# Reordering the memory stage of a fused decoder-layer kernel on all engines

## The chip, the cores and the metric

One NeuronCore of a Trainium2 chip runs the whole kernel in one launch. The metric is the device time of an execution in microseconds; lower is better.

## The reference, cut to what matters

The kernel computes one decoder layer for a prompt of 512 tokens and for 8 samples of one token each, in f32. The change touches the second part of the layer, the attention into a memory of 256 rows, with 4 heads of 256:

```python
def mem_kv(mem, mem_norm, w_mk, w_mv):
    m = rmsnorm(mem, mem_norm)
    return ((m @ w_mk).reshape(B, 256, 4, 256), (m @ w_mv).reshape(B, 256, 4, 256))

def mem_attend(h, mk, mv, w_xq, w_xo):
    q = (h @ w_xq).reshape(B, T, 4, 256)
    s = jnp.einsum('bthd,bmhd->bhtm', q, mk).astype(jnp.float32) * MEM_SCALE
    p = jax.nn.softmax(s, -1).astype(mv.dtype)
    o = jnp.einsum('bhtm,bmhd->bthd', p, mv).reshape(B, T, 1024)
    return o @ w_xo
```

The prompt's keys and values are computed here (and are outputs too). The samples read theirs from caches, 1 MB of keys and 1 MB of values for each sample.

## The kernel before, in words

**Tiling.** Every large matmul is made of three: a weight and its operand are each split into a high part (`whi`, written by ACT with a Copy) and a low part (`wlo`, written by DVE as the difference, L1756), and PE multiplies high by high, low by high and high by low (L2527 to L2529, `mm3`). So each 512 KB block of weights passes through four hands: SP loads it into one of two buffers `wraw` (`load_w`, L893, which waits until DVE has finished the low part of the block before the last), ACT writes `whi` (`split_w`, L1150, which also waits until PE has used the block three before), DVE writes `wlo`, PE multiplies. Each engine has its own list of work, written out by hand in one order, and executes it strictly in that order; semaphores tie the lists together.

**The stage.** After the query projection `xq` (eight tiles, m = 0 to 7) come 16 blocks of memory weights, called blocks 0 to 15 here. `MEM_TILES` gives their order: 0 to 3 are key tiles 0 to 3, 4 and 5 are the two halves of value tile 0, 6 and 7 are key tiles 4 and 5, 8 and 9 value tile 1, 10 and 11 key tiles 6 and 7, 12 and 13 value tile 2, 14 and 15 value tile 3. The split that stands at the head of a tile on ACT and DVE is that of a later block: `key_tile(j)` and `value_tile(h)` call `split_next`, which splits the block two further on. So `key_tile(6)` begins with the split of block 12 and `key_tile(7)` with that of block 13, on ACT and on DVE.

**The prompt's attention**, head by head, h = 0 to 3: `mem_scores(h)` on PE; `cmaxes(h)` on DVE (row maxima, value `cnegm`); `cexps(h)` on ACT; `normalised(h)` on DVE (value `cpn`); `turned(h)`: eight transposes on PE, high part `PTc_hi` on ACT, low part on DVE; `mixed(h)`: PE multiplies the values with the turned probabilities, ACT and DVE split the result into `A_hi` and `A_lo`. `key_rows(h)` turns keys back for the output. In ACT's list `cexps(1)` and `key_rows(1)` stand ahead of `turned(0)`.

**The samples' scores** are made on DVE, `scores_of(g)` for nine groups g = 0 to 8 (`SPREADS`): groups of 6 or 8 products of a cached key row with a query row (L2140). The query rows reach all partitions by DMA: ACT writes the rows of head h to DRAM (`query_rows(h)`, L1171), and POOL, in order of g, broadcasts them into one of four buffers `q_by` (`broadcast_rows`, L1124), once the scores four buffers back are made (`q_spent`). In POOL's list the zeroing of `Pv_pad` (L1135) stands at g = 3 and waits first for PE's sum of squares `("ssq", "nx")`. Scores of groups 0 to 4 stand in the `xq` loop behind the tiles m = 3 to 7, those of groups 5 to 8 behind key tiles 0 to 3. From all scores follows a small chain: `cmx` (maximum, DVE), `cmxt` (transpose, PE), `cdiag` (DVE), `cmxb` (matmul, PE), `cdif` (DVE), the exponential `Pcs` (ACT), `csum` (DVE), `ctot` (PE), `cpnorm` (DVE); then `cached_values(b)` on PE, 16 matmuls for each sample.

**SP's queue.** `load_w` of block i and the cached values share one list. The values V0 to V7 go into slots that held cached keys, so their loads wait: V0 for the scores of group 7 (`spent(sp, 7, 1)`), V1 to V3 for those of group 8 (`spent(sp, 8, 1)`), V4 and V5 for `mem_scores(1)`, V6 and V7 for `cached_values` that have freed a slot. V0 stands behind the load of block 8, V1 to V3 behind blocks 9 to 11, V4 and V5 behind 12 and 13. ACT's `mixed(0)` and `mixed(1)` wait for the scores of group 8 as well, since `A_hi` overwrites those slots.

**PSUM.** Seven banks are handed out in the fixed order of `bank_order`; PE waits for the bank seven places back to be freed.

Of the kernel before, what the change touches and what calls it, by code (L numbers as in the profile page):

```python
# [21 lines left out]
P = 128  # L22
# [3 lines left out]
NB = 8  # L26
# [67 lines left out]
def weight_pieces():  # L94

    o = []
    for j in range(J0, NF):
# [4 lines left out]
SPREADS = [[[(0, 0), (0, 1)], [(0, 2)]], [[(0, 3), (0, 4)], [(0, 5), (0, 6)]],  # L102
# [4 lines left out]
QBUF = 4  # L107

# [21 lines left out]
def bank_order():  # L130
# [59 lines left out]
        if m == 6:  # L190
            o += [("ssq", "nx")]
    o += [("mm", 0), ("qt", 3)] + [("mm", j) for j in (1, 2, 3)]
    o += mem_scores(0) + [("mn", 0)] + [("mv", 0), ("mm", 4), ("cmxt",), ("mm", 5), ("cmxb",)]
    o += mem_scores(1) + [("mn", 1)] + turned(0) + [("mv", 1), ("ctot",)] + mixed(0) + [("mm", 6), ("mm", 7)]
    o += mem_scores(2) + [("mn", 2)] + turned(1) + mem_scores(3) + [("mn", 3), ("mv", 2)] + mixed(1)
    o += turned(2) + [("mv", 3)] + mixed(2) + turned(3) + [("xo", 0, 0), ("cot",)] + mixed(3)
    o += [("xo", m, f) for m in range(KD) for f in (0, 1) if m or f]
    for j in range(J0 - 1):
# [15 lines left out]
def val_order():  # L214

    o = [("gT",), ("xsg",), ("xs1",)] + [("x1", c) for c in range(0, KD, 2)]
    o += [("ms", "n1"), ("n1d",), ("bc",)]
    o += [("ckv", r, f) for r in (0, 1) for f in (0, 1)]
    o += [("krx", f) for f in (0, 1)] + [("gT2",), ("cpT",)]
    o += [("up", g, f) for g in (3, 2) for f in (0, 1)]  # L220
    o += [("kr", f) for f in (0, 1)]
    o += [("ms", "nkv"), ("nkd",)]
    o += [("up", g, f) for g in (1, 0) for f in (0, 1)]
    o += [("c", r, f) for f in (1, 0) for r in (0, 1)]
    o += [("cq", m, f) for m in range(KQ) for f in (0, 1)]
    o += [("ms", "nq"), ("rq",)]
    o += [("qr", p, f) for p in (0, 1) for f in (0, 1)]
    o += [("qs",), ("qls",), ("sprod",)]
    us = units()
    o += [("negm",) + us[0], ("negm",) + us[1], ("negm",) + us[2], ("rs",) + us[0]]  # L230
    for n in range(len(us)):
        o += [("rs",) + v for v in us[n + 1:n + 2]] + [("negm",) + v for v in us[n + 3:n + 4]]
        if n == len(us) - 1:
            o += [("turned", 0)]
    for b in range(1, NB):
        if b in ADDED:
            o += [("xo1", ADDED[b], 0)]
        o += [("turned", b)]
    o += [("bias",), ("own_p",), ("spread_p",), ("xo1", 4, 0), ("rows",), ("xo1", 5, 0)]
    for n, m in enumerate(OUT_ORDER):  # L240
        o += [("xo1", m, f) for f in (0, 1) if f or m >= NFIRST]
        if n == MT_AT - 3:
            o += [("ms", "mem")]
        if n == MT_AT - 2:
            o += [("memn",)]
    o += [("ms", "nxs"), ("rx",), ("ms", "nx"), ("rxp",), ("cnegm", 0), ("cmx",), ("cdiag",), ("cpn", 0), ("cdif",), ("csum",)]
    o += [("cnegm", 1), ("cpn", 1), ("cpnorm",), ("cnegm", 2), ("cnegm", 3), ("cpn", 2), ("cpn", 3)]
    for m in range(KD):
        if m == 3:
            o += [("T13", J0)]  # L250
        if m == 4:
            o += [("T2", J0), ("T4", J0)]
        o += [("xo2", m, f) for f in (0, 1)]
    o += [("ms", "nf", f) for f in (0, 1)]
    for j in range(J0):
        if j == 1:
            o += [("S1",), ("S2",), ("S3",)]
        o += [("gv", j, 0)]
        if j == 0:
            o += [("xg", c) for c in range(0, 4)]  # L260
        if j == 1:
            o += [("S4",)]
        o += [("gv", j, 1)]
        if j == 0:
            o += [("xg", c) for c in range(4, KD)]
        o += [("h", j)]
    for j in range(J0, NF + 1):
        if j + 1 < NF:
            o += [("T13", j + 1), ("T2", j + 1), ("T4", j + 1)]
        if j > J0:  # L270
            o += [("u0", j - 1), ("h", j - 1)]
        if j < NF:
            o += [("u1", j), ("g0", j)]
    for m in range(KD - 1):
        o += [("xo3", m, f) for f in (0, 1)]
        if m in (5, 6):
            o += [("y", t, m - 5) for t in range(5)]
    for g in (0, 1):
        o += [("xo3", KD - 1, g), ("ms", "nz", g), ("z", g)] + [("zs",)] * g + [("yinv", g)]
        o += [("yout", t) for t in Y_GROUP[g] if t % 2 == 0]  # L280
    return o
# [61 lines left out]
def build(nc, a, consts, outs):  # L343
# [4 lines left out]
    with ctx:  # L348
# [531 lines left out]
        def _(sp):  # L880
# [60 lines left out]
            for i in range(2, len(MEM_TILES) + 2):  # L941
# [2 lines left out]
                    full(sp, ("xq", KD - 1, 1))  # L944
                    load_kv(7)
                if i == 8:
                    spent(sp, 7, 1)
                    load_kv(NB)
                elif i in (9, 10, 11):
                    spent(sp, 8, 1)  # L950
                    load_kv(NB + i - 8)
                elif i in (12, 13):
                    full(sp, ("cs", 1, 1))
                    load_kv(NB + i - 8)
                elif i in (14, 15):
                    sp.wait_ge(v_used, i - 13)
                    load_kv(NB + i - 8)
            def load_b(j):

                if j == J0 + 1:  # L960
# [28 lines left out]
        def _(gp):  # L989
# [140 lines left out]

            squares("nx", "xo1", range(KD), lambda c: xT[:, c, :], accx, sqx, between=first_rows)
            for g in range(2, len(SPREADS)):
                if g == 3:
                    full(gp, ("ssq", "nx"))
                    gp.memset(Pv_pad[:, :], 0.0).then_inc(vpad_set, 1)  # L1135
                broadcast_rows(g)
# [4 lines left out]
        def _(act):  # L1141
# [352 lines left out]
            def value_tile(h):  # L1494
# [4 lines left out]
                b = full(act, ("mv", h)).rearrange("p (t c) -> p t c", t=2)  # L1499
                act.activation(dst, b, ACT.Copy).then_inc(v_staged, 1)  # L1500
                if h == 0:
                    spent(act, 7, 1)
                else:
                    freed(act, ("cpv", h - 2, 1)) if h >= 2 else None
                high(("mv", h), mv_hi[:, h % 2, :, :], b)
# [16 lines left out]
            def turned(h):  # L1522
                for mb in (0, 1):
# [1 line left out]
                    if h and mb == 0:  # L1525
                        full(act, ("cpv", h - 1, 1))
                    if h == 0 and mb == 0:
                        spent(act, 7, 1)
                    high(("cpt", h, mb), PTc_hi[:, mb, :], b)

            def mixed(h):
# [15 lines left out]
            value_tile(0)  # L1547
            key_tile(4)
            key_tile(5)
            after(("cdif",))  # L1550
            act.activation(Pcs[:, :, :, :], Dc[:, :, :, :], ACT.Exp, scale=MEM_SCALE).then_inc(c_exp, 1)
            cexps(1)
            key_rows(1)
            turned(0)
# [1 line left out]
            mixed(0)  # L1556
            key_tile(6)
            key_tile(7)
            cexps(2)
            key_rows(2)  # L1560
            turned(1)
# [168 lines left out]
        def _(dve):  # L1730
# [420 lines left out]
            for m in range(KD):  # L2151
# [13 lines left out]
                if m == 6:  # L2165
# [3 lines left out]
                    step(dve.reciprocal(rx[:, 0:4], rx[:, 0:4]))  # L2169
                    dve.tensor_scalar(x_scale[:, 0], rx[:, 0:4], MEM_SCALE, None, ALU.mult).then_inc(rx_made, 1)  # L2170
                    value(("rxp",), dve.tensor_scalar(x_scale[:, 1], rx[:, 0:4], -MEM_SCALE, None, ALU.mult))
                if m >= 3:
                    scores_of(m - 3)


# [36 lines left out]

            for j in range(4):
                key_tile(j)
                if j == 3:
                    split_next(("mv", 0, 0))
                scores_of(5 + j)
            cmaxes(0)
            value(("cmx",), dve.tensor_reduce(cols[:, 3], Sc[:, :, :, :].rearrange("p b j h -> p b h j"), AX, ALU.max))
            split_next(("mv", 0, 1))  # L2220
            b = full(dve, ("cmxt",))
            top = cols[0:NB * NH, 2].rearrange("p b h -> p (b h)")[:, 0:1]
            frees(dve.reduce_max(top, b[0:NB * NH, 0:P], AX), ("cmxt",))
            freed(dve, ("cmxt",))
            value(("cdiag",), dve.tensor_scalar(diag[0:NB * NH, :], ident[0:NB * NH, 0:NB * NH], top, None, ALU.mult))
            value_tile(0)
            normalised(0)
            key_tile(4)
            key_tile(5)
            b = full(dve, ("cmxb",))  # L2230
            frees(dve.tensor_copy(cols[:, 3].rearrange("p b h -> p (b h)"), b[:, 0:NB * NH]), ("cmxb",))
            freed(dve, ("cmxb",))
            value(("cdif",), dve.tensor_tensor(Dc[:, :, :, :], Sc[:, :, :, :], inner(cols[:, 3], 2), ALU.subtract))
            dve.wait_ge(c_exp, 1)
            value(("csum",), dve.tensor_reduce(cols[:, 6], Pcs[:, :, :, :].rearrange("p b j h -> p b h j"), AX, ALU.add))
            cmaxes(1)
            turned(0)
            value_tile(1)
            normalised(1)
            mixed(0)  # L2240
            ins = dve.reciprocal(cols[:, 7].rearrange("p b h -> p (b h)"), full(dve, ("ctot",))[:, 0:NB * NH])
            frees(ins, ("ctot",))
            freed(dve, ("ctot",))
# [1 line left out]
            own_column = Pv_pad[:, 0:NB * (VW + 1)].rearrange("p (b x) -> p b x", x=VW + 1)[:, :, 0:VW]  # L2245
            value(("cpnorm",), dve.tensor_tensor(own_column.rearrange("p b (j h c) -> p b j h c", j=2, h=NH)[:, :, :, :, 0],
                                                 Pcs[:, :, :, :], inner(cols[:, 7], 2), ALU.mult))
            key_tile(6)
            key_tile(7)
            cmaxes(2)  # L2250
            turned(1)
            cmaxes(3)
            normalised(2)
# [247 lines left out]
        def _(pe):  # L2501
# [545 lines left out]
            key_rows(0)  # L3047
            value_tile(0)
            key_tile(4)
            b = out(("cmxt",))  # L3050
            after(("cmx",))
            filled(pe.transpose(b[0:NB * NH, 0:P], cols[:, 3].rearrange("p b h -> p (b h)"), ident[:, :]), ("cmxt",))
            key_tile(5)
            b = out(("cmxb",))
            after(("cdiag",))
            filled(pe.matmul(b[:, 0:NB * NH], ones[0:NB * NH, :], diag[0:NB * NH, :], start=True, stop=True), ("cmxb",))
            mem_scores(1)
            key_rows(1)
            turned(0)
            value_tile(1)  # L3060
            b = out(("ctot",))
            after(("csum",))
            filled(pe.matmul(b[:, 0:NB * NH], ones[:, :], cols[:, 6].rearrange("p b h -> p (b h)"), start=True, stop=True), ("ctot",))
            mixed(0)
            key_tile(6)
            key_tile(7)
            cached_values(0)
            mem_scores(2)
            key_rows(2)
            cached_values(1)  # L3070
            turned(1)
            mem_scores(3)
            key_rows(3)
            cached_values(2)
            cached_values(3)
            value_tile(2)
            mixed(1)
            cached_values(4)
            turned(2)
            value_tile(3)  # L3080
            cached_values(5)
            mixed(2)
# [203 lines left out]
```

## Time and profile before

| | us |
|---|---|
| three runs | 814.67, 818.43, 821.01 |
| median | 818.43 |
| the profiled execution, its own time | 817.74 |
| its span, first to last instruction | 815.9 |
| granted clock of PE, mean over the span | 0.986 |

The profiled execution lies 0.69 us below the median. Its span leaves 1.84 us outside. Times in rows are microseconds from the start of the span. A granted clock of 1.00 is 2.4 GHz; the lower of its two levels is 1.2 GHz, which would show as 0.50, so a mean between them is a mixture.

### The profile page before, as it was taken

To read this page: it belongs to the slowest core of one execution; us is meant where nothing else is said; L and a number is where in the kernel's file an instruction comes from. 1 tells how busy PE (TensorE), PEld (TensorE's weight loads), DVE (VectorE), ACT (ScalarE), POOL (GpSimd) and SP (SyncE) were. 2 spreads that over 40 slices of the span, in tenths; PEclk is the share of its full clock that TensorE was granted. 3 is DMA by queue.
4 is the path that set the end of the run, shared out by engine and by line. 5 is a ranking of instruction groups with operands and counts; after the bars stand their busy time and mean duration, and the time that the engine had idled before them with its cause. 6 is when DMAs were issued, how large, how long until landed. Compare 5 with 4: busy or idle time off the path is not lost. (4 is left out here: it accounts for less than half of the span.)

```text
span 815.9 us, 15998 instructions
## 1 busy us (share of the span) xinstructions
PE 770.4 (94%) x6304; PEld 736.3 (90%) x6304; DVE 550.2 (67%) x1092; ACT 378.2 (46%) x817; POOL 126.0 (15%) x179
## 2 busy tenths in 40 slices
PE   6999988988999988889999998999999999999995
PEld 6998877865899988878799998999999999999995
DVE  5678664678566779756379889888888879222323
ACT  5524775512264433655334345555555567122313
POOL 0376302331004821000046000000000000000000
PEclk9999998999999998999999999999999999999998
DMA  9323332544496658894243231433333331432312
GB/s 271 103 53 92 91 106 69 215 155 156 129 327 223 196 160 241 284 358 155 78 127 104 66 90 57 121 107 110 112 105 110 110 100 53 142 90 77 95 47 104
DMA packets 142176, 109.93 MB, mean 135 GB/s; under 512 B 9239, under 2 KB 134128, under 8 KB 139023
## 3 DMA queue, kind: packets, MB, share of 16 engines
q1 hardware_dynamic: 135239, 90.32, 36.5%
q0 software_dynamic: 3104, 14.68, 5.5%
q10 hardware_dynamic: 3760, 3.92, 1.4%
q8 instruction: 50, 0.82, 0.4%
q14 instruction: 23, 0.19, 0.1%
HBM read 103.93 MB, written 5.20 MB: 134 GB/s over the span
## 5 line engine op out<-in xcount | busy, mean ns | idle before, releaser
L1756 DVE TENSOR_TENSOR wlo<-wraw,whi 128x512 fp32r<-128x512 f32 (+1 forms) x207 | 145.7, 745 | 101.7 <-ACT whi L1150 93.3
L1150 ACT ACTIVATE whi<-wraw 128x512 fp32r<-128x512 f32 (+1 forms) x186 | 103.6, 608 | 128.7 <-PE ps L2529 80.6
L2527 PE MATMUL ps<-B_hi,whi 128*128 128x260 f32 x416 | 119.5, 287 | 3.3 <-DVE cT L1794 1.5
L2529 PE MATMUL ps<-B_hi,wlo 128*128 128x260 f32 x416 | 117.8, 283 | 0.0
L2528 PE MATMUL ps<-B_lo,whi 128*128 128x260 f32 x416 | 117.7, 283 | 0.0
L2528 PE MATMUL ps<-h_lo,whi 128*128 128x260 f32 x352 | 99.6, 283 | 0.0
L2527 PE MATMUL ps<-h_hi,whi 128*128 128x260 f32 x352 | 99.5, 283 | 0.0
L2529 PE MATMUL ps<-h_hi,wlo 128*128 128x260 f32 x352 | 99.4, 282 | 0.0
L2527 PEld LDWEIGHTS ps<-B_hi,whi 128*128 128x128 f32 x416 | 78.6, 189 | 4.6 <-issue 3.3
L2527 PE MATMUL ps<-A_hi,whi 128*128 128x260 f32 x264 | 76.0, 288 | 4.1 <-DVE A_lo L1756 2.9
L2529 PEld LDWEIGHTS ps<-B_hi,wlo 128*128 128x128 f32 x416 | 78.7, 189 | 0.0
L2528 PEld LDWEIGHTS ps<-B_lo,whi 128*128 128x128 f32 x416 | 78.6, 189 | 0.1
L2528 PE MATMUL ps<-A_lo,whi 128*128 128x260 f32 x264 | 74.5, 282 | 0.0
L2529 PE MATMUL ps<-A_hi,wlo 128*128 128x260 f32 x264 | 74.4, 282 | 0.0
L2527 PEld LDWEIGHTS ps<-h_hi,whi 128*128 128x128 f32 x352 | 66.3, 188 | 0.0
L2529 PEld LDWEIGHTS ps<-h_hi,wlo 128*128 128x128 f32 x352 | 66.3, 188 | 0.0
L2528 PEld LDWEIGHTS ps<-h_lo,whi 128*128 128x128 f32 x352 | 66.2, 188 | 0.0
L3137 PE MATMUL ps<-B_hi,whi 128*128 128x260 f32 x220 | 62.2, 283 | 1.2 <-ACT upv L1645 1.2
L3137 PE MATMUL ps<-B_lo,whi 128*128 128x260 f32 x220 | 62.1, 282 | 0.0
L3137 PE MATMUL ps<-B_hi,wlo 128*128 128x260 f32 x220 | 62.1, 282 | 0.0
L2527 PEld LDWEIGHTS ps<-A_hi,whi 128*128 128x128 f32 x264 | 49.7, 188 | 7.3 <-issue 4.3
L2528 PEld LDWEIGHTS ps<-A_lo,whi 128*128 128x128 f32 x264 | 49.7, 188 | 0.1
(476 smaller groups left out, 2057.7 us busy)
## 6 DMA issues: line engine op xcount, KB each, us to landing
kv_slot<-in_cache_mem_k_dram SPq DMA_DIRECT2D x8, 1024.0 KB, 8.9
kv_slot<-in_cache_mem_v_dram SPq DMA_DIRECT2D x8, 1024.0 KB, 7.1
wraw<-in_w_out_dram SPq DMA_DIRECT2D x14, 512.0 KB, 5.3
wraw<-in_w_down_dram SPq DMA_DIRECT2D x14, 512.0 KB, 4.0
wraw<-in_w_up_dram SPq DMA_DIRECT2D x13, 512.0 KB, 4.4
wraw<-in_w_in_dram SPq DMA_DIRECT2D x9, 512.0 KB, 4.3
xraw<-in_w_gate_dram SPq DMA_DIRECT2D x18, 256.0 KB, 3.6
xraw<-in_w_up_dram SPq DMA_DIRECT2D x9, 512.0 KB, 4.1
```

What stands on the lines that cost most here:

```text
L1150: act.activation(whi[:, home(s), c0:c1], raw(s)[:, c0:c1], ACT.Copy).then_inc(w_hi, 1)
L1756: return dve.tensor_tensor(dst, src, high.bitcast(F32), ALU.subtract)
L2527: pe.matmul(dst, left[0], right[0], start=first, stop=False)
L2528: pe.matmul(dst, left[0], right[1], start=False, stop=False)
L2529: return pe.matmul(dst, left[1], right[0], start=False, stop=last)
L3137: ins = pe.matmul(b[:, 0:TH], x[:, c], y[:, k, :], start=first and k == n == 0, stop=k == 3 and n == 2, skip_group_check=True)
```

## The change

Nothing is added to or taken from the arithmetic; instructions and waits move in the lists of all engines, and in the bank order. `scores_of(4)` to `scores_of(6)` move behind key tiles 0 to 2, `scores_of(7)` and `scores_of(8)` behind key tile 5 and value tile 1. The maximum and softmax of the samples move behind key tiles 6 and 7; `normalised(0)` moves behind key tiles 4 and 5. Groups 6 and 7 change places. SP's loads V1 to V3 move behind blocks 11 to 13, V4 and V5 behind 14 and 15, V6 and V7 behind 16 and 17 (the first two blocks of `w_xo`). POOL zeroes `Pv_pad` at g = 5. The lines left out below are the same moves in `bank_order` and `val_order`, and on ACT the `Pcs` exponential, which moves from behind key tile 5 to behind key tile 7, with `spent(act, 7, 1)` become `spent(act, 6, 1)` in `value_tile(0)` and `turned(0)`.

```diff
-           [[(0, 7), (1, 7)], [(2, 7)]], [[(3, 0), (3, 1)], [(3, 2), (3, 3)]],
+           [[(3, 0), (3, 1)], [(3, 2), (3, 3)]], [[(0, 7), (1, 7)], [(2, 7)]],
...
@@ SP @@
                 if i == 8:
-                    spent(sp, 7, 1)
+                    spent(sp, 6, 1)
                     load_kv(NB)
-                elif i in (9, 10, 11):
+                elif i in (11, 12, 13):
                     spent(sp, 8, 1)
-                    load_kv(NB + i - 8)
-                elif i in (12, 13):
+                    load_kv(NB + i - 10)
+                elif i in (14, 15):
                     full(sp, ("cs", 1, 1))
-                    load_kv(NB + i - 8)
-                elif i in (14, 15):
-                    sp.wait_ge(v_used, i - 13)
-                    load_kv(NB + i - 8)
+                    load_kv(NB + i - 10)
+                elif i in (16, 17):
+                    sp.wait_ge(v_used, i - 15)
+                    load_kv(NB + i - 10)
@@ POOL @@
-                if g == 3:
+                if g == 5:
                     full(gp, ("ssq", "nx"))
                     gp.memset(Pv_pad[:, :], 0.0).then_inc(vpad_set, 1)
@@ DVE @@
-                if m >= 3:
+                if 3 <= m < 7:
                     scores_of(m - 3)
...
             for j in range(4):
                 key_tile(j)
-                if j == 3:
-                    split_next(("mv", 0, 0))
-                scores_of(5 + j)
+                if j < 3:
+                    scores_of(4 + j)
+            split_next(("mv", 0, 0))
             cmaxes(0)
+            split_next(("mv", 0, 1))
+            value_tile(0)
+            key_tile(4)
+            key_tile(5)
+            normalised(0)
+            scores_of(7)
+            cmaxes(1)
+            turned(0)
+            value_tile(1)
+            scores_of(8)
             value(("cmx",), ...)
-            split_next(("mv", 0, 1))
+            mixed(0)
+            key_tile(6)
             b = full(dve, ("cmxt",))
...
             value(("cdiag",), ...)
-            value_tile(0)
-            normalised(0)
-            key_tile(4)
-            key_tile(5)
+            normalised(1)
+            key_tile(7)
             b = full(dve, ("cmxb",))
...
             value(("csum",), ...)
-            cmaxes(1)
-            turned(0)
-            value_tile(1)
-            normalised(1)
-            mixed(0)
+            cmaxes(2)
...
-            key_tile(6)
-            key_tile(7)
-            cmaxes(2)
             turned(1)
@@ PE @@
             key_tile(4)
-            b = out(("cmxt",))
...
             key_tile(5)
-            b = out(("cmxb",))
...
             mem_scores(1)
             key_rows(1)
             turned(0)
             value_tile(1)
+            mixed(0)
+            key_tile(6)
+            b = out(("cmxt",))
+            after(("cmx",))
...
+            key_tile(7)
+            b = out(("cmxb",))
+            after(("cdiag",))
...
+            mem_scores(2)
+            key_rows(2)
             b = out(("ctot",))
             after(("csum",))
...
-            mixed(0)
-            key_tile(6)
-            key_tile(7)
-            cached_values(0)
-            mem_scores(2)
-            key_rows(2)
-            cached_values(1)
             turned(1)
             mem_scores(3)
             key_rows(3)
+            cached_values(0)
+            cached_values(1)
+            value_tile(2)
+            mixed(1)
             cached_values(2)
             cached_values(3)
-            value_tile(2)
-            mixed(1)
+            turned(2)
             cached_values(4)
-            turned(2)
             value_tile(3)
             cached_values(5)
             mixed(2)
```

## Rows read from the trace of the kernel before

**Rows 1.** The page: busy time of each engine over the span.
```profile
PE 770.4 (94%) x6304; PEld 736.3 (90%) x6304; DVE 550.2 (67%) x1092; ACT 378.2 (46%) x817; POOL 126.0 (15%) x179
```
**Rows 2.** PE's timeline in the stage: start, duration, in brackets idle and releaser.
```profile
305.55 0.59 PE L2945 MATMUL ps<-ident,qcs 128*8 128x128 f32 x2 [2.27 <-DVE qcs L2163]
...
315.06 0.39 PE L2527 MATMUL ps<-mT_hi,whi 128*128 128x256 f32 x1 [2.06 <-DVE wlo L1756]
...
332.74 0.27 PE L3052 MATMUL ps<-ident,cols 128*32 128x128 f32 x1 [1.25 <-DVE cols L2219]
...
349.87 0.80 PE L2527 MATMUL ps<-PTc_hi,mv_hi 128*128 128x512 f32 x1 [2.62 <-DVE PTc_lo L1756]
...
359.75 1.07 PE L3037 MATMUL ps<-kv_slot,Pv_pad 128*32 128x256 f32 x16
...
371.46 0.38 PE L2992 MATMUL ps<-whi,mT_hi 128*128 128x256 f32 x1
...
401.42 0.39 PE L2527 MATMUL ps<-A_hi,whi 128*128 128x260 f32 x1 [1.48 <-DVE A_lo L1756]
```
**Rows 3.** Windows: us, then busy PE, PEld, DVE, ACT, POOL; granted clock, DMA share, GB/s.
```profile
315.00:320.00 5.00, 4.94 (x28) 4.94 (x29) 4.79 (x19) 1.84 (x4) 1.08 (x2) 0.66 0.85 300
...
335.00:340.00 5.00, 5.00 (x42) 4.82 (x41) 3.01 (x5) 4.43 (x10) 0.00 (x0) 1.00 1.00 305
...
350.00:355.00 5.00, 5.00 (x19) 4.13 (x20) 4.74 (x8) 3.15 (x7) 0.00 (x0) 0.69 0.85 270
```
**Rows 4.** DVE's timeline: scores of group 3, a weight split, steps of head 0 and 1.
```profile
299.94 0.43 DVE L2140 CUSTOM_DVE_ANT_0 prod<-kv_slot,q_by 128x256 f32<-128x256 f32 x1 [3.40 <-DMA q_by<-q_rows]
...
303.69 1.29 DVE L1756 TENSOR_TENSOR wlo<-wraw,whi 128x512 fp32r<-128x512 f32 x2
...
336.96 0.69 DVE L1756 TENSOR_TENSOR mv_lo<-ps,mv_hi 128x512 fp32r<-128x512 f32 x1 [2.71 <-ACT mv_hi L1156]
...
337.77 1.23 DVE L2203 TENSOR_TENSOR Pc<-Pc,cstat 128x1024 f32<-128x1024 f32 x1
...
342.89 1.41 DVE L2195 TENSOR_REDUCE cstat<-ps 128x2 f32<-128x512 f32 x2
...
352.14 0.69 DVE L1756 TENSOR_TENSOR mv_lo<-ps,mv_hi 128x512 fp32r<-128x512 f32 x1
```
**Rows 5.** POOL's timeline: the broadcasts of query rows and the zeroing.
```profile
285.48 1.12 POOL L1124 DMA_DIRECT2D q_by<-q_rows  x2 [0.30 <-POOL accx L1014]
294.66 0.56 POOL L1135 MEMSET Pv_pad<- 128x552 f32 x1 [8.07 <-PE ps L2964]
295.17 2.13 POOL L1124 DMA_DIRECT2D q_by<-q_rows  x4
...
312.95 0.54 POOL L1124 DMA_DIRECT2D q_by<-q_rows  x1 [3.44 <-DMA q_rows<-q_nat]
```
**Rows 6.** ACT's timeline: query rows of head 3, splits of blocks 3, 7, 13, exponentials.
```profile
306.75 0.27 ACTq L1171 DMA_DIRECT2D q_rows<-q_nat  x1
311.15 1.16 ACT L1150 ACTIVATE whi<-wraw 128x512 fp32r<-128x512 f32 x2 [4.44 <-DMA wraw<-in_w_mk_dram]
...
328.66 1.16 ACT L1150 ACTIVATE whi<-wraw 128x512 fp32r<-128x512 f32 x2 [2.27 <-DMA wraw<-in_w_mk_dram]
...
332.49 0.56 ACT L1517 ACTIVATE Pc<-ps,cstat,x_scale 128x256 f32<-128x256 f32 x1 [1.38 <-DVE cstat L2196]
...
359.58 1.15 ACT L1150 ACTIVATE whi<-wraw 128x512 fp32r<-128x512 f32 x2 [1.53 <-DMA wraw<-in_w_mv_dram]
```
**Rows 7.** SP's timeline: loads of blocks 6 and 7 (merged), block 12, V4, block 13.
```profile
319.38 5.65 SPq L893 DMA_DIRECT2D wraw<-in_w_mk_dram  x2
...
351.05 0.37 SPq L893 DMA_DIRECT2D wraw<-in_w_mv_dram  x1
351.46 0.50 SPq L926 DMA_DIRECT2D kv_slot<-in_cache_mem_v_dram  x1
352.25 0.37 SPq L893 DMA_DIRECT2D wraw<-in_w_mv_dram  x1
```

More of the change, by code:

```diff
@@ L192, in bank_order @@
     o += [("mm", 0), ("qt", 3)] + [("mm", j) for j in (1, 2, 3)]
-    o += mem_scores(0) + [("mn", 0)] + [("mv", 0), ("mm", 4), ("cmxt",), ("mm", 5), ("cmxb",)]
-    o += mem_scores(1) + [("mn", 1)] + turned(0) + [("mv", 1), ("ctot",)] + mixed(0) + [("mm", 6), ("mm", 7)]
-    o += mem_scores(2) + [("mn", 2)] + turned(1) + mem_scores(3) + [("mn", 3), ("mv", 2)] + mixed(1)
+    o += mem_scores(0) + [("mn", 0), ("mv", 0), ("mm", 4), ("mm", 5)]
+    o += mem_scores(1) + [("mn", 1)] + turned(0) + [("mv", 1)] + mixed(0) + [("mm", 6), ("cmxt",), ("mm", 7), ("cmxb",)]
+    o += mem_scores(2) + [("mn", 2), ("ctot",)] + turned(1) + mem_scores(3) + [("mn", 3), ("mv", 2)] + mixed(1)
     o += turned(2) + [("mv", 3)] + mixed(2) + turned(3) + [("xo", 0, 0), ("cot",)] + mixed(3)
@@ L245, in val_order @@
             o += [("memn",)]
-    o += [("ms", "nxs"), ("rx",), ("ms", "nx"), ("rxp",), ("cnegm", 0), ("cmx",), ("cdiag",), ("cpn", 0), ("cdif",), ("csum",)]
-    o += [("cnegm", 1), ("cpn", 1), ("cpnorm",), ("cnegm", 2), ("cnegm", 3), ("cpn", 2), ("cpn", 3)]
+    o += [("ms", "nxs"), ("rx",), ("ms", "nx"), ("rxp",), ("cnegm", 0), ("cpn", 0), ("cnegm", 1), ("cmx",), ("cdiag",)]
+    o += [("cpn", 1), ("cdif",), ("csum",), ("cnegm", 2), ("cpnorm",), ("cnegm", 3), ("cpn", 2), ("cpn", 3)]
     for m in range(KD):
@@ L1501, in value_tile @@
                 if h == 0:
-                    spent(act, 7, 1)
+                    spent(act, 6, 1)
                 else:
@@ L1527, in turned @@
                     if h == 0 and mb == 0:
-                        spent(act, 7, 1)
+                        spent(act, 6, 1)
                     high(("cpt", h, mb), PTc_hi[:, mb, :], b)
@@ L1549, in _ @@
             key_tile(5)
-            after(("cdif",))
-            act.activation(Pcs[:, :, :, :], Dc[:, :, :, :], ACT.Exp, scale=MEM_SCALE).then_inc(c_exp, 1)
             cexps(1)
@@ L1558, in _ @@
             key_tile(7)
+            after(("cdif",))
+            act.activation(Pcs[:, :, :, :], Dc[:, :, :, :], ACT.Exp, scale=MEM_SCALE).then_inc(c_exp, 1)
             cexps(2)
@@ L3049, in _ @@
             key_tile(4)
-            b = out(("cmxt",))
-            after(("cmx",))
-            filled(pe.transpose(b[0:NB * NH, 0:P], cols[:, 3].rearrange("p b h -> p (b h)"), ident[:, :]), ("cmxt",))
             key_tile(5)
-            b = out(("cmxb",))
-            after(("cdiag",))
-            filled(pe.matmul(b[:, 0:NB * NH], ones[0:NB * NH, :], diag[0:NB * NH, :], start=True, stop=True), ("cmxb",))
             mem_scores(1)
@@ L3060, in _ @@
             value_tile(1)
+            mixed(0)
+            key_tile(6)
+            b = out(("cmxt",))
+            after(("cmx",))
+            filled(pe.transpose(b[0:NB * NH, 0:P], cols[:, 3].rearrange("p b h -> p (b h)"), ident[:, :]), ("cmxt",))
+            key_tile(7)
+            b = out(("cmxb",))
+            after(("cdiag",))
+            filled(pe.matmul(b[:, 0:NB * NH], ones[0:NB * NH, :], diag[0:NB * NH, :], start=True, stop=True), ("cmxb",))
+            mem_scores(2)
+            key_rows(2)
             b = out(("ctot",))
```

## The prediction, made before the changed kernel ran

> **What bounds the kernel now.** The page comes first: PE is busy for 94% of the span [rows 1], so a gain can only come from the gaps in PE's list, and a loss only from new ones. PE's own timeline between 300 and 402 us then gives the gaps of the memory stage [rows 2]: 2.27, 2.06, 1.25, 2.62 and 1.48 us, 9.7 us together. The reader is to see who ended each: DVE every time, once with the samples' query columns (`qcs`), once with the low part of a weight block (block 3), once with the maximum of the samples' scores (`cols`), twice with low parts of the attention. So DVE's list, with the scores in it, paces PE here. The windows [rows 3] show a second price: behind the 2.06 us gap the granted clock is 0.66 over 5 us, and behind the 2.62 us gap 0.69, that is a mixture of the 1.2 and 2.4 GHz levels that loses 5 x 0.34 = 1.7 and 5 x 0.31 = 1.5 us; behind the 1.25 us gap it stayed at 1.00. A gap above 2 us thus costs about 1.5 us more than itself.
>
> DVE's timeline says why it is late: it stood 3.40 us for query rows of group 3, then did 8 products in 303.69 - 299.94 = 3.75 us (0.47 each), and only then split block 1 [rows 4]. POOL says why the rows were late: it was ready at 286.6, stood 8.07 us for PE's sum of squares ahead of the zeroing, and issued the rows of group 3 at 295.17 [rows 5]; they landed 4.8 us later.
>
> **The change, part by part.** I follow DVE, ACT, SP and PE through the new lists with durations of the rows. Nothing computed is added, so the sum of instructions is zero everywhere; only gaps count.
>
> *POOL's zeroing later.* Rows of group 3 can be issued once the scores of group 1 are made (8 products from 285.2, so near 289; the first half near 287) and land by about 294. DVE then starts group 3 at 296.5, when its preceding work ends, not at 299.94: 3.4 us earlier. It could also gain nothing, if something else holds the rows; bounds 0 and -3.4, and I take -3.4 because POOL's wait is a row with its cause. The zeroing itself (0.56 us) has 50 us to spare.
>
> *Group 4 behind the first key tile.* DVE: group 3 to 300.2, block 1's split (1.21) to 301.4, lows of the last `xq` tile to 302.2. The columns are there before PE has done key tile 0 at 303.3, so the 2.27 us gap goes. Block 2's split to 303.4, low part to 304.5 (it waits for PE and ACT), group 4 (6 products, 2.8) to 307.3. Block 3's load is issued at 301.5 and lands 6.2 us later as before (304.9 to 311.15, [rows 4, 6]) at 307.7; with ACT's first half, DVE has split it at 309.5. PE is done with key tile 2 at 309.4: the 2.06 us gap goes, and the low clock with it. PE's head start is now 7 us.
>
> *What is late next.* Group 5 to 313.8, block 4 to 315.0. Group 6 is now head 3, whose rows ACT writes at 304.7 (306.75 before); they took 6.2 us to POOL's issue at 312.95 [rows 5, 6], so the broadcast goes out at 310.9 and lands at 315.8. Group 6 to 319.6, block 5 to 320.8. PE wants block 5 at 319.0: gap 1.8, in place of the 1.25. Block 7's load is issued behind block 5's split, 320.9, and lands 4.0 us later (324.66 to 328.66, [rows 6, 7]). ACT splits it and loads its table: before, it was ready at 332.49 - 1.38 = 331.1, 2.4 us after the landing, and then stood for `cnegm` [rows 6]. Now it is ready at 327.3 and doesn't stand, since `cmaxes(0)` (1.41 and a small product, [rows 4]) is done at 324.7. Exponentials, key rows and value tile took from 332.49 to 336.9, 4.4 us. So DVE gets value tile 0 at 331.7, 5.2 us earlier than 336.96 [rows 4].
>
> *`normalised(0)` behind key tiles 4 and 5.* ACT's next two splits and copies end 3.6 us later (335.3); DVE's `normalised(0)` ends at 337.0 (1.35 with its reciprocal, [rows 4]). PE is done with `key_rows(1)` at 333.5: a new gap of 3.6 us with its low clock. Group 7 (2.8) and `cmaxes(1)` (1.6) follow on DVE to 341.4. From the end of `cmaxes(1)` (342.89 + 1.6 = 344.5) to PE's `mixed(0)` it took 5.4 us [rows 2, 4], through ACT's exponentials, `key_rows(1)` and `turned(0)`; so `mixed(0)` is now at 346.8. PE, in value tile 1 until 345, waits 1.8 more. The head start has shrunk to 3 us.
>
> *Groups 8, SP's wait and block 12.* Low of value tile 1 ends 2.9 us after `mixed(0)` begins (349.87 to 352.74), now at 349.7; group 8 (3.75) to 353.5. Three things wait for it: ACT's `mixed(0)`, the maximum `cmx`, and SP. SP stands at V1, and behind V1 in its list are blocks 12 and 13. Block 12 could have been issued at 348, when block 10 is split; it goes at 354.1, behind V1's issue of 0.5. `key_tile(6)` on DVE begins with the split of block 12, and behind that split stand `cmxt`'s maximum and `cdiag`, for which PE waits ahead of `cmxb`. How long block 12 takes is not in the trace in this surrounding. The nearest rows bound it: block 7, with nothing just ahead of it, took 4.0 us, and block 13, behind block 12 and V4, took 7.3 us (352.25 to 359.58, [rows 6, 7]). With one MB ahead and V2 close behind I take 6.0, nearer to 7.3, since V1 is as large as V4. It lands at 360.1; ACT and DVE split it to 361.9; low of key tile 6, maximum and `cdiag` to 362.9.
>
> PE: `mixed(0)` to 351.2 (4.4 at the low clock, as before), key tile 6 to 354.1, transpose, key tile 7 to 357.2. Then it stands until 362.9: 5.7 us, the largest gap of the stage, and a low clock behind it (1.5).
>
> *The rest.* `mem_scores(2)` to 367.7, `key_rows(2)`, `ctot`, `turned(1)` to 369.4, `mem_scores(3)` and `key_rows(3)` to 373.0, cached values 0 and 1 (1.07 each, [rows 2]) to 375.1. Block 13 lands at 362.7, `csum` is ready at about 366.6; neither is late. Value tile 2 began at 371.46 with four cached values done [rows 2]; now it begins at 375.1 with two. Lag: 3.6 + 2 x 1.05 = 5.7 us. Behind it the loads V4 to V7 have 6 us and more to spare, PE works without gaps as before, and the 1.48 us gap at the end of head 3 stays, its chain untouched. The rest shifts as a whole.
>
> **The sum.** Gains: 2.27 + 2.06 + 1.25 + 2.62 = 8.2 of gaps and 3 x 1.5 of clock (one for each gap above 2 us), 12.7. Losses: 1.8 + 3.6 + 1.8 + 5.7 = 12.9 of gaps and 3 x 1.5 of clock (`turned(0)`, `mixed(0)`, `cmxb`), 17.4. Difference +4.7; following the lists gives +5.7, since my hand reading rounds some twenty steps, and small waits that are no row of mine are in it. I take the latter: 817.74 + 5.7 = 823.4 for the profiled execution, and 824.1 from the median of 818.43.
>
> The Trainium skill, "DMA: Bandwidth & Descriptors", section "Queues, rings and completion order", says that each DMA engine consumes a ring's descriptors in order. By that, V2 and V3 behind block 12 would not delay it and only V1's MB would, and block 13's 7.3 us behind 1.5 MB of others agrees with it. Block 13 had 1.5 MB ahead and 0.5 of its own, block 12 would have 1 MB and 0.5, so by the rule an estimate is 7.3 x 1.5 / 2 = 5.5 us and a sum of +5.2; by the row of block 13 alone it would be +7.0.
>
> **The rivals.**
> *A. The head start is kept (faster).* PE is 7 us ahead at 333. If block 12 is no wait, the gap at `cmxb` (5.7) and its clock (1.5) go, and if ACT's stretch behind block 7 is shorter than I read, `turned(0)` and `mixed(0)` come 3 us earlier: 5.7 - 7.2 - 3.0 = -4.5, 814. For it: the gaps removed are rows with causes. Against: SP's list puts V1, and the wait for group 8, ahead of block 12. It decides at `cmxb`: begun before 357.5, this holds.
> *B. Gaps only move (no change).* The losses are half of what I sum, as the slow stretches fall into waits anyway: +1, 819. For it: DVE's work between 296 and 362 is the same. Against: two serial chains were lengthened by scores.
> *C. Slower still.* The rows of group 3 or of head 3 come late (their priority on POOL does not help, or queues are fuller): the 3.4 us come back through every step to block 12, and its landing takes 7.3: 5.7 + 3.4 + 1.3 = +10.4, 829.
> *D. The change does nothing for the gaps on DVE.* If PE's first two gaps stay and all else too, the same path as C with 3.4 only: 827.5. I count it with C.
>
> **How the numbers follow.** My forecast, one long gap at `cmxb`: 0.45, own range 820 to 828 from the landing of block 12 (-2.0 to +1.3), the clock (-1.5) and my reading of some twenty steps (2 us). A 0.2, B 0.17, C with D 0.18. The range 811 to 830 holds nearly all of B, and of A and C what lies within 3 us above or below their values on the near side. A measurement of this kernel tells about 1%, 8.2 us, from no change: faster by more needs under 810.2, slower over 826.6. From the forecast a quarter lies above 826.6 (0.11), from C nearly all (0.16): 0.27 slower. Faster: a quarter of A (0.05) and 0.09 for a step I misread near the first gaps, 0.14. The rest, 0.59, is within 1%.
>
> **What would show it.** POOL issues the rows of group 3 near 287 and 289, and DVE has no gap ahead of group 3. PE has no gap at `qcs` and none at block 3; a gap of 3 to 4 us at `turned(0)` ended by `Pc`; a gap of 4 to 7 us at `cmxb` ended by `diag`, with SP's load of block 12 just behind V1 and ACT's split of block 12 ended by DMA. A clock below 0.8 in the 5 us behind each. Wrong would be: `cmxb` without a gap above 2 us, or value tile 2 begun before 371, or new gaps behind 380 us.

## The result and the profile after

The changed kernel takes 827.47 us (median of 4 runs, 824.09 to 829.38) against 816.55 us (4 runs) of the kernel before: ratio 1.0109, 95% interval 1.0079 to 1.0139. In the later comparisons, with 11 to 21 runs each, the kernel before had medians of 818.3 to 818.5, so the loss is 9 to 11 us. The forecast was 824.1. Two executions far above all others, 1917.49 us of the kernel before and 3755.99 us of the variant with only the splits moved, are left out of every median here. The profiled execution of the changed kernel took 829.38 us (span 827.6).

PE does the same work, in a longer span [rows 1]. Its 774.5 us of busy time are 4.1 more than before, though the instructions are the same, since a matmul at the low clock takes longer (128x256 behind `turned(0)`: 0.41 us for 0.28):

```profile
PE 774.5 (94%) x6304; PEld 740.9 (90%) x6304; DVE 549.3 (66%) x1092; ACT 377.3 (46%) x817; POOL 124.4 (15%) x179
```

PE's timeline of the changed kernel in the stage, to be laid beside [rows 2]: start, duration, in brackets the idle time before and what ended it.

```profile
305.61 0.38 PE L2947 MATMUL ps<-ident,qcs 128*8 128x128 f32 x2 [1.16 <-DVE qcs L2163]
...
312.83 0.39 PE L2529 MATMUL ps<-mT_hi,whi 128*128 128x256 f32 x1 [1.20 <-DVE wlo L1756]
...
323.39 0.38 PE L2994 MATMUL ps<-whi,mT_hi 128*128 128x256 f32 x1 [1.33 <-DVE wlo L1756]
...
327.13 0.38 PE L2529 MATMUL ps<-mT_hi,whi 128*128 128x256 f32 x1 [0.73 <-DVE wlo L1756]
...
340.94 1.97 PE L3018 MATMUL ps<-ident,Pc 128*128 128x128 f32 x8 [4.03 <-DVE Pc L2203]
...
350.58 0.50 PE L2529 MATMUL ps<-PTc_hi,mv_hi 128*128 128x512 f32 x1 [1.60 <-DVE PTc_lo L1756]
...
357.55 0.27 PE L3061 MATMUL ps<-ident,cols 128*32 128x128 f32 x1 [1.10 <-DVE cols L2229]
...
366.68 0.60 PE L3065 MATMUL ps<-diag,ones 32*128 32x32 f32 x2 [5.94 <-DVE diag L2236]
...
410.80 0.39 PE L2529 MATMUL ps<-A_hi,whi 128*128 128x260 f32 x1 [1.85 <-DVE A_lo L1756]
```

With one more of 0.39 at 330.6 the gaps between 296 and 415 us sum to 19.3 us; before, the same sum is 10.5, with a sixth gap of 0.84 at 333.85 that [rows 2] leave out. The first two gaps are shorter than before (1.16 and 1.20 for 2.27 and 2.06), `mixed(0)` at 350.58 too (1.60 for 2.62). Two are new: 4.03 us at `turned(0)`, released by `Pc`, which is `normalised(0)`, and 5.94 us at `cmxb`, released by `diag`. The windows of 5 us of the changed kernel (length, PE, PEld, DVE, ACT and POOL busy, granted clock, DMA share, GB/s) show the low clock behind both, and behind the last gap, where it had not been before:

```profile
340.00:345.00 5.00, 4.06 (x24) 4.06 (x25) 4.76 (x15) 0.00 (x0) 0.00 (x0) 0.66 0.45 130
...
365.00:370.00 5.00, 3.32 (x15) 3.29 (x16) 4.39 (x11) 2.43 (x6) 0.00 (x0) 0.50 1.02 385
...
410.00:415.00 5.00, 4.20 (x23) 4.20 (x24) 2.23 (x4) 1.14 (x3) 0.61 (x1) 0.70 0.28 75
```

By the reading of the prediction (5 us times what is missing to 1.00) these lose 1.7, 2.5 and 1.5 us. The 2.5 contain idle time, since 1.7 us of that window belong to the gap itself; 3.32 us of busy time at 0.50 lose 1.7, and the next window, at 0.90, 0.5 more. Behind `mixed(0)` the clock stays at 1.00.

Where the two profiled executions part can be read from two instructions that both have. PE's sum of squares ahead of the stage begins at 293.65 before and at 294.82 now, and the last gap ends at 401.42 and at 410.80. So of the 11.7 us between the spans 1.2 are there ahead of the stage, 8.2 arise in it, and 2.3 behind its last gap.

Where the 5.94 us come from stands in SP's and ACT's timelines: V1 is issued when the scores of group 8 are made, block 12 just behind it, and ACT stands 5.49 us until block 12 lands. DVE had finished the low part of block 10, for which block 12 has to wait in any case, at about 351.7 (an estimate: two of the four halves that its timeline merges into 2.49 us from 350.44); the other 5.9 us SP stood for group 8.

```profile
357.17 0.34 SPq L926 DMA_DIRECT2D kv_slot<-in_cache_mem_v_dram  x1
357.56 0.43 SPq L893 DMA_DIRECT2D wraw<-in_w_mv_dram  x1
358.04 0.50 SPq L926 DMA_DIRECT2D kv_slot<-in_cache_mem_v_dram  x1
```

On ACT:

```profile
363.75 1.15 ACT L1150 ACTIVATE whi<-wraw 128x512 fp32r<-128x512 f32 x2 [5.49 <-DMA wraw<-in_w_mv_dram]
```

Block 12 took 6.2 us from issue to use; the forecast had 6.0. On POOL the two halves of the rows of group 3 go out as soon as each half of group 1 is done, and DVE's timeline has no wait ahead of group 3 any more, where [rows 4] had 3.40 us:

```profile
291.19 0.54 POOL L1124 DMA_DIRECT2D q_by<-q_rows  x1 [2.19 <-DVE Sc L2140]
293.06 0.54 POOL L1124 DMA_DIRECT2D q_by<-q_rows  x1 [1.33 <-DVE Sc L2140]
```

and on DVE:

```profile
299.94 0.16 DVE L2171 TENSOR_SCALAR x_scale<-rx 128x4 f32<-128x4 f32 x1
300.01 0.42 DVE L2140 CUSTOM_DVE_ANT_0 prod<-kv_slot,q_by 128x256 f32<-128x256 f32 x1
```

Yet group 3 begins at 300.01, not earlier than the 299.94 of before. In this execution DVE's work ahead of it was 3.6 us later: group 0 began at 280.89 and not at 277.32, since its rows came later by DMA (PE itself was 1.2 us later), in a part of the lists that the change does not touch. Over the 14 profiled executions of this study that start lies anywhere between 275.3 and 280.9, with no relation to the edits that can be seen. So absolute starts of two single profiles must not be compared in this stage; gaps and medians can.

### The profile page after: what moved, and what is told of

Same layout as the page of the kernel before. It is cut to its first block and busy times, and to the rows that moved or that the text cites. A ratio compares the mean times of both kernels' runs of the same rounds, so it can differ in the third digit from the quotient of the medians.

```text
span 827.6 us, 15997 instructions
## 1 busy us (share of the span) xinstructions
PE 774.5 (94%) x6304; PEld 740.9 (90%) x6304; DVE 549.3 (66%) x1092; ACT 377.3 (46%) x817; POOL 124.4 (15%) x179
```

## The experiments

Theory 1 says that the loss sits in two serial chains that the new order made longer: SP's wait for group 8 ahead of block 12, and DVE's scores and splits ahead of head 0's softmax. Theory 2 says that DVE's total work paces the stage, so that gaps only move.

The ratios are against the kernel before, with their 95% intervals. The differences from the changed kernel are differences of medians, and less sure: it has only four executions, from 824.09 to 829.38, and by the spread of the runs such a difference is known to about 4 us either way. Only that of the three edits together (5.1), and that of the variants built on it, are clear of this; for the others the gaps in the traces carry the argument.

### Blocks 12 and 13 ahead of V1

```diff
-                elif i in (11, 12, 13):
+                elif i in (13, 14, 15):
                     spent(sp, 8, 1)
-                    load_kv(NB + i - 10)
+                    load_kv(NB + i - 12)
...
```

The lines left out move V4 and V5 behind blocks 16 and 17, and V6 and V7 behind V5.

> The changed kernel with SP's loads of blocks 12 and 13 put ahead of V1 (V1 to V3 behind blocks 13 to 15, V4 and V5 behind 16 and 17, V6 and V7 last). Theory 1 (the loss is SP's wait for the scores of group 8 ahead of block 12): block 12 is issued near 351 instead of 357.6, ACT's split of it doesn't wait for DMA, PE's gap at cmxb falls from 5.9 us to about 1.5, its low clock goes, and the time falls by 5 to 7 us, to about 821. Theory 2 (DVE's total of work paces the stage and gaps only move): the gap at cmxb falls but as much comes back at csum, turned(1) or the values; time within 2 us of 827.5.

Measured: 823.18 us, ratio 1.0072 (1.0046 to 1.0098), 4.3 us under the changed kernel. SP now issues block 12 at 348.93:

```profile
348.93 0.37 SPq L893 DMA_DIRECT2D wraw<-in_w_mv_dram  x1
```

PE's timeline of this kernel:

```profile
358.48 0.37 PE L3067 MATMUL ps<-diag,ones 32*128 32x32 f32 x2 [0.57 <-DVE diag L2238]
...
382.92 1.93 PE L3041 MATMUL ps<-kv_slot,Pv_pad 128*32 128x256 f32 x16 [2.71 <-DMA kv_slot<-in_cache_mem_v_dram]
```

The 5.94 us are 0.57. A new gap of 2.71 us comes from DMA: V4, which now stands behind block 16, is late. So SP's order is shown as the cause of the largest gap. What it is worth in time is less sure: 4.3 us by the medians. In the two profiled executions PE comes from its sum of squares to `cmxb` 5.7 us sooner (66.15 us for 71.86) and gives 4.0 of them back from there to the end of the last gap (48.16 for 44.12), through V4 and a clock of 0.50 in the 5 us behind it.

### `cdiag` ahead of key tile 6 on DVE

```diff
             mixed(0)
-            key_tile(6)
             b = full(dve, ("cmxt",))
...
             value(("cdiag",), ...)
+            key_tile(6)
             normalised(1)
```

> The changed kernel with the maximum over cmxt and cdiag put ahead of key tile 6 on DVE, so that they don't stand behind the split of block 12; block 12 is as late as before. Theory 1: the gap at cmxb goes to under 1 us, but normalised(1) and mem_scores(3) still stand behind blocks 12 and 13, so that PE, 4 us further on, waits at turned(1) or at csum; the time falls by only 2 to 4 us. Theory 2: within 2 us of 827.5.

Measured: 830.31 us, ratio 1.0147 (1.0128 to 1.0166), 2.8 us above the changed kernel, not under it. The gap at `cmxb` is gone, and PE's timeline of this kernel has one at `ctot`:

```profile
370.87 0.61 PE L3070 MATMUL ps<-cols,ones 128*128 128x32 f32 x2 [7.46 <-DVE cols L2244]
```

On ACT, the split of block 13:

```profile
367.50 1.15 ACT L1150 ACTIVATE whi<-wraw 128x512 fp32r<-128x512 f32 x2 [3.23 <-DMA wraw<-in_w_mv_dram]
```

`csum` stands on DVE and ACT behind key tile 7, and that behind block 13, which lands after block 12. Freed at `cmxb`, PE runs two pieces of work further and then waits for the later block, 7.46 us in one piece. The 2 to 4 us that theory 1 expected did not come; a loss is not shown, since 2.8 us lie within what the changed kernel's four runs leave open. With the blocks late, it doesn't help to change which instruction meets the wait.

### `normalised(0)` ahead of key tiles 4 and 5

```diff
             value_tile(0)
+            normalised(0)
             key_tile(4)
             key_tile(5)
-            normalised(0)
             scores_of(7)
```

> The changed kernel with normalised(0) back ahead of key tiles 4 and 5 on DVE. Theory 1: PE's gap at turned(0) falls from 4.0 us to under 1 and its low clock (about 1.5 us) goes, but mixed(0) waits for a chain through cmaxes(1) that is not earlier, so nearly all of it comes back as a longer gap at mixed(0): time down by 0 to 2 us. Rival (PE's gap at turned(0) is paid in full): down by 4 to 5.5 us.

Measured: 826.96 us, ratio 1.0099 (1.0075 to 1.0124), 0.5 us under the changed kernel. PE's timeline of this kernel:

```profile
335.52 0.66 PE L3018 MATMUL ps<-ident,Pc 128*128 128x128 f32 x4 [0.60 <-DVE Pc L2203]
...
348.25 0.79 PE L2529 MATMUL ps<-PTc_hi,mv_hi 128*128 128x512 f32 x1 [5.74 <-DVE PTc_lo L1756]
```

The gap at `turned(0)` went from 4.03 to 0.60, and the one at `mixed(0)` grew from 1.60 to 5.74. The sum of the two is 5.6 before the edit and 6.3 behind it: `mixed(0)` has its own chain, and PE waits for it if it did not wait ahead of it.

### The three edits together

Blocks 12 and 13 ahead of V1, `cdiag` ahead of key tile 6, and `normalised(0)` ahead of key tiles 4 and 5.

> The three edits together (blocks 12 and 13 ahead of V1, cdiag ahead of key tile 6, normalised(0) ahead of key tiles 4 and 5). Theory 1: no gap above 2 us is left but that at mixed(0); time 7 to 10 us under the changed kernel, 818 to 820, about the kernel before. Theory 2: within 3 us of 827.5.

Measured: 822.41 us (7 runs), ratio 1.0062 (1.0038 to 1.0086): 5.1 us under the changed kernel, less than the 7 to 10 expected, and 4 us above the kernel before. Gaps of 5.7 us at `mixed(0)` and 2.7 us for V4 are left.

### ... and ACT's `turned(0)` ahead of its exponentials

```diff
+            turned(0)
             cexps(1)
             key_rows(1)
-            turned(0)
             value_tile(1)
```

> The kernel of the three edits together, with one more: on ACT turned(0) ahead of cexps(1) and key_rows(1). That kernel's largest gap left was 5.7 us ahead of mixed(0), with a low clock behind it, made by the chain cmaxes(1), exponentials, turned(0). If so, most of it goes: 3 to 6 us off 822.4, to 816.5 to 819.5. If DVE's turned(0), which still stands behind group 7 and cmaxes(1), sets the gap, only 2.7 us (the exponentials and key rows) come off it, with the low clock staying, and the time is 820.

Measured: 821.49 us, ratio 1.0051 (1.0031 to 1.0071). PE's timeline of this kernel:

```profile
342.91 0.50 PE L2531 MATMUL ps<-PTc_hi,mv_hi 128*128 128x512 f32 x1 [1.61 <-DVE PTc_lo L1758]
...
346.99 0.39 PE L2531 MATMUL ps<-mT_hi,whi 128*128 128x256 f32 x1 [1.03 <-DVE wlo L1758]
...
352.94 0.27 PE L3063 MATMUL ps<-ident,cols 128*32 128x128 f32 x1 [2.85 <-DVE cols L2231]
...
381.27 1.07 PE L3041 MATMUL ps<-kv_slot,Pv_pad 128*32 128x256 f32 x16 [2.27 <-DMA kv_slot<-in_cache_mem_v_dram]
```

`mixed(0)` fell from 5.7 to 1.6, but a gap of 2.85 us opened at `cmxt`, which waits for `cmx`, and that for group 8. The time moved by 0.9 us, which can't be told from nothing, and the sum of all gaps from 13.3 to 13.0. At this place it is as theory 2 says: DVE makes the scores of group 8 and `cmx` without a wait from 348.85 to 352.8, so PE's gap ends with DVE's work.

### ... and V4 one block earlier

> As the run before, with V4 loaded behind block 15 and V5 behind block 16 instead of one block later each. In the kernels with blocks 12 and 13 ahead of V1 PE stood 2.7 us for V4; if SP's list made that, the gap goes and the time falls by 2 to 3 us more. If PE has slack there, within 1 us.

Measured: 820.13 us (12 runs), ratio 1.0018 (0.9998 to 1.0037), 1.4 us less than the run before, again within the spread. In PE's timeline of this kernel no wait for DMA is left; the gap at `cmxt` is the largest:

```profile
352.43 0.27 PE L3065 MATMUL ps<-ident,cols 128*32 128x128 f32 x1 [2.96 <-DVE cols L2233]
```

### The zeroing on POOL, both ways

The changed kernel with `if g == 3`, and the kernel before with `if g == 5`:

> The changed kernel with POOL's zeroing back at g = 3, so that the rows of group 3 wait for PE's sum of squares. Theory 1 (the earlier rows are worth their 3.4 us all the way down the chain): DVE stands about 3 us ahead of group 3 again, PE's gap at qcs grows by as much, and the time rises by 3 to 4 us over the changed kernel. Theory 2 (a wait further down takes it up): within 1 us of the changed kernel.

> The kernel before with only POOL's zeroing moved to g = 5. Theory 1: no gap of DVE ahead of group 3, PE's gaps at qcs (2.27) and block 3 (2.06) shrink by 2 us or go with their low clock; time down by 2 to 4 us from the kernel before. Theory 2 (block 3's landing sets the next gap anyway): down by under 1 us.

Measured: 830.41 us, ratio 1.0143 (1.0122 to 1.0164), 2.9 us above the changed kernel; and 815.14 us (12 runs), ratio 0.9954 (0.9936 to 0.9971), 3.3 us under the kernel before. In the first, DVE's timeline has a wait ahead of group 3 again, though of 1.72 us and not of 3:

```profile
300.03 0.43 DVE L2140 CUSTOM_DVE_ANT_0 prod<-kv_slot,q_by 128x256 f32<-128x256 f32 x1 [1.72 <-DMA q_by<-q_rows]
```

PE's gaps at `qcs` and block 3 grow from 1.16 and 1.20 to 1.54 and 1.99. In PE's timeline of the second there is no gap at `qcs` (2.27 before); block 3 keeps one of 2.19 (2.06 before):

```profile
312.81 0.39 PE L2527 MATMUL ps<-mT_hi,whi 128*128 128x256 f32 x1 [2.19 <-DVE wlo L1756]
```

One line of the change is thus worth 3.3 us in the kernel before, shown by 12 runs. In the changed kernel its 2.9 us agree but are not shown by themselves: they are within the spread of its four runs, and the gaps named grow by 1.2 us together. The whole change is slower in spite of this line: without it, it is 12 us slower than the kernel before.

### The splits ahead of the scores alone

```diff
-                if m >= 3:
+                if 3 <= m < 7:
                     scores_of(m - 3)
...
-                scores_of(5 + j)
+                scores_of(4 + j)
+            scores_of(8)
             cmaxes(0)
```

This is the kernel before, with groups 4 to 7 one step later.

> The kernel before with only the splits ahead of the scores: groups 4 to 7 behind key tiles 0 to 3 and group 8 behind group 7. Theory 1: blocks 1 to 3 are split 2.8 us earlier, the gap at qcs shrinks to nothing or little since the columns come without group 4 ahead, the gap at block 3 falls by 2; DVE's total ahead of cmx is the same, so that the later gaps stay: time down by 1 to 3 us. Theory 2 (scores anywhere cost the same): within 1 us of the kernel before.

Measured: 824.29 us (5 runs), ratio 1.0066 (1.0049 to 1.0083): 5.8 us slower, where 1 to 3 us of gain had been expected. PE's timeline of this kernel:

```profile
335.71 0.37 PE L3053 MATMUL ps<-ident,cols 128*32 128x128 f32 x1 [5.83 <-DVE cols L2220]
```

The windows:

```profile
330.00:335.00 5.00, 0.00 (x0) 0.00 (x0) 4.65 (x20) 1.50 (x2) 0.00 (x0) 1.00 0.63 218
335.00:340.00 5.00, 3.55 (x16) 3.28 (x17) 2.23 (x8) 3.99 (x12) 0.00 (x0) 0.52 0.40 143
340.00:345.00 5.00, 5.00 (x33) 4.80 (x33) 4.97 (x10) 3.44 (x8) 0.00 (x0) 0.80 0.96 300
```

PE runs ahead of key tiles 0 to 4 and then waits for the maximum over all scores in one gap of 5.83 us, with no matmul at all between 330 and 335 and a clock of 0.52 and 0.80 behind it. DVE is no faster: from its last step ahead of group 3 (L2171) to the end of `cmaxes(0)` it takes 36.5 us here and 36.1 before. Several gaps became one, and the one costs the clock more than each of them. That is why the change moves the maximum as well; but then groups 7 and 8 fall into head 0.

### ACT's `turned(0)` first, in the kernel before

> The kernel before with one edit on ACT: turned(0) ahead of cexps(1) and key_rows(1). If the gap ahead of mixed(0) is made by ACT's exponentials standing ahead of the turned probabilities, the 2.62 us gap goes and its low clock (1.5) with it: time down by 3 to 4 us. If cexps(1), now later, holds something else on PE (bank of cs), it comes back: within 1 us.

Measured: 816.08 us (12 runs), ratio 0.9974 (0.9962 to 0.9986), 2.4 us faster. The 2.62 us gap at `mixed(0)` is gone; no new gap takes its place.

### Both gains together, and the smallest form of the idea

> The kernel before with two edits that were each faster alone: POOL's zeroing at g = 5 (-3.5 us) and ACT's turned(0) ahead of cexps(1) (-2.5 us). They act on different gaps of PE (qcs at 305, mixed(0) at 350), so the gains should add: 812 to 813.5, the fastest so far. If one chain serves both, 815.

Measured: 813.14 us (7 runs), ratio 0.9938 (0.9915 to 0.9961): 5.3 us faster than the kernel before, 14 us faster than the changed one, and within the spread the sum of the two single gains (5.7). Its largest gaps in PE's timeline:

```profile
312.31 0.39 PE L2527 MATMUL ps<-mT_hi,whi 128*128 128x256 f32 x1 [2.19 <-DVE wlo L1756]
...
331.52 0.27 PE L3052 MATMUL ps<-ident,cols 128*32 128x128 f32 x1 [2.39 <-DVE cols L2219]
```

On top of it, with `cmxt` behind key tile 5, `cmxb` behind `mem_scores(1)`, and block 7 split ahead of `cmaxes(0)`:

> The fastest kernel so far (813.1: the kernel before with the zeroing at g = 5 and ACT's turned(0) first) with the idea of the change in its smallest form: PE's cmxt moves behind key tile 5 and cmxb behind mem_scores(1), and DVE splits block 7 ahead of cmaxes(0); no scores, no cached values move. If a wait of PE is removed by moving only what waits for it, the gaps of 2.4 us at cmxt and 0.8 us at key tile 5 shrink to under 1 us together and turned(0), whose chain comes 1.2 us later, takes at most 1 us back: time down by 1 to 3 us, 810 to 812. If PE's head start is lost at turned(0) in full, as in the changed kernel: within 1 us.

Measured: 813.80 us, ratio 0.9951 (0.9936 to 0.9967): no difference that can be told from 813.14. The 1 to 3 us expected did not come. The 2.39 us went, and PE met the chain at the next waits, as its timeline in this kernel shows:

```profile
328.20 0.38 PE L2527 MATMUL ps<-mT_hi,whi 128*128 128x256 f32 x1 [1.93 <-DVE wlo L1756]
...
336.26 0.66 PE L3016 MATMUL ps<-ident,Pc 128*128 128x128 f32 x4 [0.68 <-DVE Pc L2203]
```

## Why the prediction was right, and what was mis-sized

The direction and the mechanism held; the size did not: +5.7 us was forecast, 9 to 11 were measured. The measured 827.5 us lie even above the 826.6 that the prediction gave a chance of 0.27 to be passed.

- *POOL's zeroing*: forecast -3.4, measured -3.3 in the kernel before; the 2.9 us of it within the change are not clear of the spread. Right in sum.
- *The 2.27 us gap goes, the 2.06 us gap goes*: half right. They shrank to 1.16 and 1.20. The term that was mis-sized is the head start of DVE, "group 3 at 296.5", taken from the single profile of before. Against PE's sum of squares, which is part of PE's own list, group 3 should have begun 2.85 us later (296.5 and 293.65); in the changed kernel it was 5.19. This distance varies from execution to execution. In the variants whose lists are the same up to there it was 2.65, 2.78 and 2.79 us in three, and neither gap is there; it was 3.96, 4.13 and 4.61 in the others, and a gap of 1.2 to 2.1 us stands at block 3. So the reading of the two gaps is confirmed where the start was as read.
- *All later steps*: from group 3 on every landmark came 3.5 to 3.9 us behind its forecast: `turned(0)` at 340.94 for 337.0, `mixed(0)` at 350.58 for 346.8, block 12 issued at 357.56 for 354.1, `cmxb` at 366.68 for 362.9, value tile 2 at 378.60 for 375.1. The path between them was read rightly, and the 3.5 us of group 3 run through it. Only block 13 came later still, its split at 367.75 for a landing at 362.7; that made no gap here, but it is the block that PE waits for once `cdiag` is moved.
- *The gap at value tile 0, 1.8*: 1.33, but followed by 0.73 and 0.39 at key tiles 4 and 5, and by 1.10 at `cmxt`. The last three are not in the forecast, nor are the 1.16 and 1.20 above; these five make 4.6 us, nearly all that was missing in the sum of gaps (12.9 forecast, 17.5 measured without the last).
- *3.6 at `turned(0)`*: 4.03. *1.8 at `mixed(0)`*: 1.60. *5.7 at `cmxb`, because block 12 stands behind V1*: 5.94, and the experiment that puts block 12 ahead of V1 takes it to 0.57. *6.0 us for block 12*: 6.2. Right, each within 0.5 us. The sequence rule drawn from the Trainium skill, "DMA: Bandwidth & Descriptors", section "Queues, rings and completion order", gave an estimate of 5.5; the measurement lies between that and the row of block 13.
- *Three losses of 1.5 us of clock*: three were seen, but not the three that were named. `mixed(0)`, whose 1.8 us lie under the 2 us of the prediction's own reading, had 1.00 behind it; the last gap, for which nothing was counted, had 0.70. That the number of losses fits is luck.
- *The 1.48 us gap at the end stays, its chain untouched*: wrong by size. It is 1.85 us in the changed kernel, 0.37 more. The same 1.85 stand in all eight profiles of the changed kernel and its variants, and in the kernel before with only the splits moved; the other five have 1.48. In the first group DVE's last `A_lo` begins 0.46 or 0.47 us behind the end of ACT's `A_hi`, in the second 0.10. The low clock is a matter of the execution: 0.66 over the 5 us behind the end of the gap in four of the nine with 1.85, 1.00 in five.
- *V4 to V7 have 6 us to spare*: no gap came from them in the changed kernel, but V4 became one of 2.7 us as soon as blocks 12 and 13 were put ahead of V1.
- *Rival A* is refuted at its own point of decision: `cmxb` did not begin before 357.5. *Rival B*, no change because gaps only move, is refuted as a whole by the measured loss (at least 0.8%), and by the 3.3 us of POOL's line, but it describes three experiments (`cdiag`, `normalised(0)`, `cmxt`), in which a gap moved on in full. *Rival C* had the size (829) and half its cause: the head start was lost early, though not by late rows of group 3.

What stays open: the last 1.7 us of the variant with all repairs against the kernel before (1.0018, interval reaching 0.9998). It contains both gains of 5.3 us and lies 7.0 us above the kernel that has those gains alone (820.13 and 813.14), so it still carries about 7 us of loss. The experiments leave for it the scores of groups 7 and 8 in head 0 and the larger last gap, but no run moved those scores back alone. Why DVE begins its last `A_lo` 0.37 us later in one group of kernels is not known.

## What to carry to other kernels

Where engines work through fixed lists as here, a gap is worth removing only if the chain that ends the next gap gets shorter too: follow it to the next wait before moving work, and look at the gap that stands there afterwards. A wait in a queue of loads holds every load behind it; put small loads that the critical engine needs ahead of a large one that has to wait. The gains here came from single instructions that stood in front of others for no need (a zeroing ahead of a broadcast, exponentials ahead of a copy for PE), 3.3 and 2.4 us each, while the large reordering lost 9 to 11.

## What was unexpected in the hardware

A gap does not cost the clock in proportion to its length. Read over the 5 us behind the end of each gap of this stage, in all 14 profiled executions, the granted clock was 1.00 behind every gap from 0.97 to 1.64 us. Behind gaps of 1.85 to 2.4 us it was 0.66 to 0.68 in some and 1.00 in others: the same 1.85 us gap at the end of head 3 had 0.66 in four executions and 1.00 in five, and 2.19 us had 0.66 twice and 1.00 once. Behind gaps of 2.6 to 3.0 us it was 0.50 to 0.68 each time. So the reading of the prediction, 1.5 us more for a gap above 2 us, does not hold for each gap; and several short gaps cost less than one long gap of the same sum: in the kernel with only the splits moved, the gap of 5.83 us was followed by 0.52 over 3.55 us of busy time and by 0.80 over the next 5 us, 2.7 us lost.

And a DMA of 8 KB of query rows, issued 1.2 us apart in two executions (270.97 and 272.14), released POOL 1.9 and 3.4 us later. So POOL issued the broadcasts 2.7 us later (275.58 for 272.84), and DVE began group 0 3.6 us later, in a part of the kernel where both lists are the same.
